# SyncE turns a head's attention probabilities ahead of a weight load instead of behind it, and weight splits run four units ahead in place of five

## The reference

```
qb, kb, vb = fox parts of h @ w_in_2
c = cumsum(log_sigmoid(f_logit))
s[t, s'] = q[t] . k[s'] / sqrt(128) + c[t] - c[s'],  s' <= t
p = softmax(s);  o = p @ v
```

## Time and profile before

| | before |
|---|---|
| median of three runs | 1051.59 us |
| the profiled execution | 1051.89 us |
| its span | 1050.1 us |
| busy: TensorE | 1043.1 us, 99% |
| busy: VectorE | 754.2 us, 72% |
| busy: ScalarE | 598.5 us, 57% |
| granted TensorE clock, mean | 0.999 |

### The profile page before, as it was taken

The page is one execution under the profiler, slowest core; times in us unless marked ns, Lnnn a source line. Parts: engine busy times, 40 slices in busy tenths (PEclk is TensorE's granted clock), DMA queues, the critical chain, the costliest instruction groups (busy, mean ns, idle before and its releaser), DMA issues.

```text
span 1050.1 us, 12969 instructions
## 1 busy us (share of the span) xinstructions
PE 1043.1 (99%) x4939; PEld 872.3 (83%) x4939; DVE 754.2 (72%) x901; ACT 598.5 (57%) x800; POOL 84.7 (8%) x91
## 2 busy tenths in 40 slices
PE   9999999999999999999999999999999999999997
PEld 7888888888888888888888888888889988888886
DVE  5768777775787675468888978868788666767642
ACT  6573776765385555448784645555366657565531
POOL 1200000000000000000444501400000000000000
PEclk9999999999999999999999999999999999999999
DMA  9945889995487877558867745879976345777741
GB/s 353 400 135 172 298 303 300 294 266 188 184 279 232 244 237 234 199 178 277 250 182 234 242 161 171 249 257 332 312 243 196 115 169 203 242 245 229 244 163 40
DMA packets 97229, 242.84 MB, mean 231 GB/s; under 512 B 15456, under 2 KB 41232, under 8 KB 97040
## 3 DMA queue, kind: packets, MB, share of 16 engines
q1 hardware_dynamic: 92576, 229.42, 67.0%
q0 software_dynamic: 4160, 12.28, 3.4%
q10 hardware_dynamic: 432, 0.33, 0.1%
HBM read 219.43 MB, written 21.50 MB: 229 GB/s over the span
## 4 chain that ended last, share of the span: by engine, by line
PE 98%; DVE 1%; ACT 0%; issue 0%; DVEq 0%
PE ps L823 24%; PE ps L824 24%; PE ps L825 24%; PE ps L862 5%; PE ps L860 5%; PE ps L861 5%; PE ps L957 1%; PE ps L1147 1%; PE ps L1258 1%; PE ps L1257 1%; PE ps L1256 1%; PE ps L1008 1%; PE ps L1009 1%; PE ps L920 1%; PE ps L919 1%; PE ps L918 1%
## 5 line engine op out<-in xcount | busy, mean ns | idle before, releaser
L1967 DVE TENSOR_TENSOR rest<-raw,high 128x2048 fp32r<-128x2048 f32 x129 | 296.2, 2312 | 77.2 <-ACT high L1371 76.6
L823 PE MATMUL ps<-high,xt_high 128*128 128x512 f32 x824 | 324.4, 394 | 0.2 <-DVE rest L1967 0.2
L824 PE MATMUL ps<-rest,xt_high 128*128 128x512 f32 x824 | 320.8, 389 | 0.0
L825 PE MATMUL ps<-high,xt_rest 128*128 128x512 f32 x824 | 320.8, 389 | 0.0
L1371 ACT ACTIVATE high<-raw 128x2048 fp32r<-128x2048 f32 x129 | 244.4, 1911 | 70.1 <-DMA raw<-in_units_dram 66.5
L825 PEld LDWEIGHTS ps<-high,xt_rest 128*128 128x128 f32 x824 | 154.7, 188 | 32.4
L823 PEld LDWEIGHTS ps<-high,xt_high 128*128 128x128 f32 x824 | 154.8, 188 | 32.0 <-DVE rest L1967 0.6
L824 PEld LDWEIGHTS ps<-rest,xt_high 128*128 128x128 f32 x824 | 154.8, 188 | 30.8
L1972 DVE SCALAR_TENSOR_TENSOR rest<-raw,wgain,high 128x512 fp32r<-128x512 f32 x176 | 119.0, 746 | 35.5 <-ACT high L1375 35.5
L1375 ACT ACTIVATE high<-raw,wgain 128x512 fp32r<-128x512 f32 x176 | 110.9, 716 | 9.4 <-DMA raw<-in_units_dram 9.4
L1631 ACT ACTIVATE act<-ps,recips 128x256 f32<-128x256 f32 x44 | 18.5, 471 | 85.0 <-PE ps L825 85.0
(11 more groups left out here) (373 smaller groups left out, 1458.5 us busy)
## 6 DMA issues: line engine op xcount, KB each, us to landing
raw<-in_units_dram SPq DMA_DIRECT2D x350, 512.0 KB, 4.8
gv_turned<-gv_blocked SPq DMA_DIRECT2D x11, 512.0 KB, 5.0
gv_t<-gv_turned SPq DMA_DIRECT2D x44, 128.0 KB, 4.2
turned<-blocked SPq DMA_DIRECT2D x22, 256.0 KB, 5.3
hid_t<-turned SPq DMA_DIRECT2D x88, 64.0 KB, 4.1
fox_turned<-fqT SPq DMA_DIRECT2D x6, 512.0 KB, 3.9
raw<-in_units_dram SPq DMA_DIRECT2D x8, 256.0 KB, 4.8
fqT<-fox_turned SPq DMA_DIRECT2D x16, 128.0 KB, 4.2
```

The lines of the kernel that those rows point to most:

```text
L823: pe.matmul(out, sh, wh, start=first, stop=False)
L824: pe.matmul(out, sh, wr, start=False, stop=False)
L825: mm = pe.matmul(out, sr, wh, start=False, stop=last)
L1967: vec.tensor_tensor(rest[:, slot, c], raw[:, slot, c], high[:, slot, c].bitcast(F32), ALU.subtract).then_inc(unit_rest, 1)
```

## The change

Two things change. On SyncE the read of head h's probabilities is moved from behind the load of unit 113 + h to ahead of it; the store of head h stays where it was, at the end of the load of unit 112 + h. A head's read thus comes directly behind its store. On ScalarE and VectorE the splits run one unit less far ahead from late in the stage: ScalarE from step 26 on, VectorE from step 23 on, four units for five. Nothing else is changed, and no work is added or taken away.

```diff
             def load(u):
 
+                read_probabilities(u - UNIT["win2"] - 33)
                 slot = u % SLOTS
...
                 turn_tokens(u)
-                turn_probabilities(u)
+                store_probabilities(u - UNIT["win2"] - 32)
...
-            def turn_probabilities(u):
-
-                h = u - UNIT["win2"] - 33
+            def read_probabilities(h):
+
                 if 0 <= h < HH:
                     sync.wait_ge(fp_stored, 16 * (h + 1))
...
-                h += 1
+
+            def store_probabilities(h):
+
                 if 0 <= h < HH:
                     sync.wait_ge(fp_blocked, h + 1)
...
-                split_to(UNIT["win2"] + u + 5)
+                split_to(UNIT["win2"] + u + (5 if u < 26 else 4))
...
-                    split_to(UNIT["win2"] + u + (4 if 5 < u < 9 or 20 < u < 23 else 3 if 8 < u < 21 else 5))
+                    split_to(UNIT["win2"] + u + (5 if u < 5 else 3 if 8 < u < 21 else 4))
```

## The result

The changed kernel takes 1054.01 us in the median of 21 runs (1051.69 to 1056.40), the kernel before 1052.20 us in the median of 21 runs on the same chips (1051.46 to 1054.14). The ratio is 1.0016, with a 95% interval of 1.0009 to 1.0023. So the change makes the kernel slower by some 1.7 us. That is just inside the 0.2% that I had named as hardly measurable, yet the interval excludes no change, and the time lies above the range that I gave. The profiled execution took 1053.91 us with a span of 1052.1, 2.0 us more than before.

The account below looks back on a forecast made before the run. TensorE was taken to bound the kernel. Read, loads and splits each added 0, at most 0.2 us gained, giving 1051.7 to 1051.9 profiled; with the median 0.3 below, forecast 1051.6 us, range 1050.9 to 1052.8.

Parts of the forecast that it names:

- What bounds the kernel: Whole kernel: TensorE sets the end, busy 1043.1 of 1050.1 us; only 0.2 us of its waiting could be gained.
- The base: Time of the kernel before: profiled execution 1051.89 us, median of the runs 0.3 below it, taken as 1051.6.
- The splits: ScalarE and VectorE, four units ahead: first maxima about 2.5 us sooner, unit 119's split hidden in idle time, 0 on TensorE's path.
- my two ends of 0 and 2.5: Lead of `at_rest`, operand of unit 116, 2.0 us before TensorE's use: gain between 0 and 2.5 us, taken as 0.
- The read's landing: SyncE's reads of probabilities, issued directly behind the stores: they come sooner and widen the lead over TensorE, worth 0.
- The tight end of 0.7 us: Fifth head's read in the old order: landed at 679.6, TensorE multiplies at 680.35, leaving 0.7 us.
- The failed step: SyncE's stores of probabilities: with no load behind, each lands in 1.9 us, the shortest landing, for all heads.
- the ends: Bounds of a store's landing time on SyncE: 1.9 us at best and 5.4 at worst, median 2.0.
- the round that I set at 4.9 us: SyncE's store, landing, read and load per head: 4.9 us against a period of 7.0, 2.1 to spare.
- The first rival: Slower: SyncE's 8.4 us rounds add up, unit 120's load comes too late, TensorE loses 3.0 us, total 1054.6; chance 0.05.
- The rule: Start a DMA early, wait late: against the read's move on SyncE, eight loads 3.4 us later, 27 us exposed, 1079.

## Why the prediction was wrong

**What bounds the kernel**: right. TensorE sets the end, and the loss is three starts of TensorE.

**The base** was 0.6 us too low. I took 1051.6 from three runs; 21 give 1052.20. Of the 2.4 us between my forecast and 1054.01 only 1.8 are the change. With the right base the range would have ended at 1053.4, still below the result.

**The splits**: right. VectorE's idle time of 4.03 us is gone; it takes the first maxima at 632.86 and the first store is issued at 636.54 (forecast near 636.5). Unit 119's split runs on VectorE from 700.30 to 702.58 (forecast 700 to 702.3) and what is behind, L2677, starts at 705.43 against 705.10. `at_rest` starts 1.5 us sooner, between my two ends of 0 and 2.5. By itself the edit measures 0.9998.

**The read's landing**: right in its sign, off TensorE's path: median 1.9 us, longest 3.1, against 3.9 and 7.2. The tight end of 0.7 us was read too tight: a landing counts from the start of its issue, 671.81 for the fifth head's last DMA and not 672.43, so it landed at 679.0 and the lead was 1.4.

**The failed step** is the one on the store: "With no load behind the store I take the shortest landing, 1.9, for all heads". I looked at what stands behind the store in the queue and not at what stands ahead of it. In the new order the load that used to follow the store precedes the next one, by 0.04 us once SyncE is late. The measured landing is 2.2, 1.9 and 3.2 us for the first three heads, 4.1 for the fourth and 5.2 to 5.6 for the rest. So the round that I set at 4.9 us, "with 2.1 us to spare", is 7.9 to 8.7 us from the fourth read on. The median of 2.0, which I let decide between the ends, was the median of the old order, in which a store waited for its probabilities and so mostly found the load ahead of it landed or about to land; SyncE waited 21.2 us in all for probabilities before, 10.4 after.

**The first rival** was the right mechanism, with a chance of 0.05. Its round of 8.4 us, 1.4 per head beyond the period, is close to what happened (8.1, that is 1.2 more than before). "Against it: they came with a load right behind the store, which is what goes away" is the sentence that set it aside, and it is the failed step again; the earlier trace rows spoke against it, where the first store has a load right behind it and the read starts 1.9 us after the store. Its place was wrong too: unit 120's load was 9.8 us late, not over 15, its split could begin on ScalarE at 704.29, and VectorE's half ended at about 711.2, some 5 us ahead of TensorE's first use of that unit, 716.11 (715.71 before). The cost fell on two things whose leads I had not read: the last head's read, 6.4 us late, and the turn of the memory behind `brB`, where the lead had been 0.14 us. Its price, 3.0 us, was nearer to the measured 1.8 than the forecast's 0, but by luck: it was worked out for unit 120, which cost nothing.

**The rule** that I weighed against the edit pointed the right way: that of the Trainium skill, "DMA: Bandwidth & Descriptors", section "Rules for kernel authors", start early and wait late. At its full size, 27 us exposed, it was far off; the measured loss is 1.8. On the failed step the same page of the Trainium skill says more, in its section "Queues, rings and completion order": a DMA's semaphore increment lands only after every earlier write of the same DMA engine, across its queues. By that a store's landing counts from the end of the load ahead of it, whatever its size and whichever queue issues it, and I had not used it. The traces agree: landings 0.5 to 0.8 us behind the load's in the changed kernel, 0.2 for the last three stores of a third of the size and for ScalarE's slowest.

**What stays open**: how the 1.8 us of the medians divide. The profile gives, in order of time, 0.29 for the last read, 0.93 more for the memory's turn and 0.60 more at a place that also loses time without the change.

## What to carry to other kernels

When a wait is moved to an in-order queue, write out the new order of that queue for two full rounds and price each DMA with what stands directly ahead of it there, not with the median of the order that is being given up. If the round comes out near the period, take the slow value: the queue that fell behind here issued everything back to back, and that was the condition in which its stores landed slowest. And follow lateness to the end of the leads: unit 120 was safe here by some 5 us, a product some 20 us behind it had 0.14.

## What was not expected of the hardware

- A 192 KB store issued 0.04 us behind a 1 MB load on the same queue landed in 5.2 to 5.6 us; with no load under way ahead of it, but one right behind, in 1.9 (first store). With 64 KB the median was 4.4 in place of 4.6.
- Issued on ScalarE's queue it still took up to 6.3 us and landed 0.2 us behind the load that SyncE had issued before it, so the load delays it across queues.
- What the stretch up to 690 us lost of DMA traffic (233 to 188 GB/s) came later, in a stretch that was busy already: behind 690 us the rate went from 293 to 327 GB/s and the share from 0.83 to 0.88, and a load there took up to 13.0 us to land (8.7 before).
